# Two of the four weight-block sums of each seven-product slot made by adding loads instead of VectorE

## What is computed

```
for l in range(2):
    x = x + rms_norm(concat(conv, retention, moba, pool) @ w_out[l], attn_post_g[l])
    h = rms_norm(x, ffn_pre_g[l])
    f = silu(h @ w_gate[l]) * (h @ w_up[l])          # 1024 -> 2816, twice
    x = x + rms_norm(f @ w_down[l], ffn_post_g[l])
```

## Time and profile before

| | us |
|---|---|
| median of 3 runs | 1066.26 |
| profiled execution, its own time | 1066.48 |
| its span | 1064.7 |
| PE busy | 1044.1 (98%) |
| DVE busy | 797.5 (75%) |
| ACT busy | 498.3 (47%) |
| POOL busy | 5.2 (0%) |
| DMA queue of SP, share of 16 engines | 31.6% |

### The profile page before, as it was taken

The page is one execution under the profiler, slowest core; times in us unless marked ns, Lnnn a source line. Parts: engine busy times, 40 slices in busy tenths (PEclk is TensorE's granted clock), DMA queues, the critical chain, the costliest instruction groups (busy, mean ns, idle before and its releaser), DMA issues.

```text
span 1064.7 us, 19739 instructions
## 1 busy us (share of the span) xinstructions
PE 1044.1 (98%) x7894; PEld 776.4 (73%) x7894; DVE 797.5 (75%) x1605; ACT 498.3 (47%) x928; POOL 5.2 (0%) x18
## 2 busy tenths in 40 slices
PE   8999999999999999999999999999999999999997
PEld 5988895587888887444488888747878888864443
DVE  6999988989899987222679888898889999761014
ACT  5545454645555666122244463465555555651000
POOL 1000000000000000000000000000000000000000
PEclk9999999999999999999999999999999999999999
DMA  9612311222333546332032140223133333560001
GB/s 338 194 64 81 118 64 57 82 79 81 118 120 120 159 121 220 135 119 79 1 107 93 41 145 15 80 80 119 41 100 113 109 136 119 165 214 18 1 20 60
DMA packets 58187, 109.84 MB, mean 103 GB/s; under 512 B 7024, under 2 KB 7280, under 8 KB 57968
## 3 DMA queue, kind: packets, MB, share of 16 engines
q1 hardware_dynamic: 58096, 108.58, 31.6%
HBM read 106.46 MB, written 2.10 MB: 102 GB/s over the span
## 4 chain that ended last, share of the span: by engine, by line
PE 88%; DVE 7%; ACT 3%; issue 1%; DMA 1%; SPq 0%; ACTq 0%; DVEq 0%
PE ps L565 52%; PE ps L672 28%; PE ps L569 3%; DVE ring L1391 2%; PE ps L831 1%; ACT ring L901 1%; PE ps L815 1%; DVE E L1505 1%; DVE hT L1513 1%; PE ps L750 1%; DMA xs<-x_dram 1%; DVE ps L1470 0%; PE ps L735 0%; ACT gbc L901 0%; PE ps L792 0%
## 5 line engine op out<-in xcount | busy, mean ns | idle before, releaser
L565 PE MATMUL ps<-ring,U 128*128 128x512 f16 x1440 | 313.4, 379 | 0.0
L1391 DVE SCALAR_TENSOR_TENSOR ring<-raw,ring 128x512 f16<-128x512 f32 (+1 forms) x300 | 210.2, 744 | 89.9 <-ACT ring L901 89.9
L565 PEld LDWEIGHTS ps<-ring,U 128*128 128x128 f16 x1440 | 140.8, 98 | 166.7 <-issue 0.3
L901 ACT ACTIVATE ring<-raw 128x512 f16<-128x512 f32 (+1 forms) x300 | 181.0, 670 | 83.6 <-PE ps L565 77.1
L565 PE MATMUL ps<-hT,ring 128*128 128x256 f16 (+1 forms) x1632 | 195.3, 279 | 0.3 <-DVE hT L1513 0.3
L565 PEld LDWEIGHTS ps<-hT,ring 128*128 128x128 f16 x1632 | 159.3, 98 | 29.4 <-DVE hT L1513 0.6
L672 PE MATMUL ps<-E,ring 128*128 128x256 f16 x1224 | 145.7, 273 | 3.8 <-ACT ps L901 3.8
L672 PE MATMUL ps<-hT,ring 128*128 128x256 f16 x1224 | 145.4, 273 | 0.0
L565 PE MATMUL ps<-ring,hT 128*128 128x256 f16 x1152 | 134.8, 275 | 0.7 <-DVE hT L1513 0.7
L672 PEld LDWEIGHTS ps<-E,ring 128*128 128x128 f16 x1224 | 117.8, 98 | 20.6 <-ACT ps L901 5.4
L672 PEld LDWEIGHTS ps<-hT,ring 128*128 128x128 f16 x1224 | 119.8, 98 | 13.8
(11 more groups left out here) (134 smaller groups left out, 857.7 us busy)
## 6 DMA issues: line engine op xcount, KB each, us to landing
raw<-weights_dram SPq DMA_DIRECT2D x368, 256.0 KB, 2.9
gbc<-gains_dram SPq DMA_DIRECT2D x8, 512.0 KB, 6.4
xs<-x_dram SPq DMA_DIRECT2D x4, 512.0 KB, 6.5
U<-weights_dram SPq DMA_DIRECT2D x8, 256.0 KB, 7.4
out_dram<-xs SPq DMA_DIRECT2D x8, 256.0 KB, 2.0
cst<-consts_dram SPq DMA_DIRECT2D x1, 1296.0 KB, 12.0
bd<-pool_w_dram SPq DMA_DIRECT2D x8, 16.0 KB, 10.0
par<-params_dram SPq DMA_DIRECT2D x1, 76.0 KB, 6.3
```

The costliest lines, as they stand in the source:

```text
L565: ins = mm(dst, st, mv_, start=first and i == 0, stop=last and i == 2, **kw)
L901: return A(dst, src, ACT.Copy, scale=scale)
L1391: V.scalar_tensor_tensor(out=at[1], in0=src, scalar=W_SCALE, in1=at[0], op0=ALU.mult, op1=ALU.subtract).then_inc(lo_split, 1)
```

## The change

In each fast slot, X1 and X2 are no longer made by DVE. X1: after part B has landed in its place in `raw`, GpSimd issues a load of part A from DRAM onto the same place with an add (`accum_op`). X2: SP loads part B a second time, into one of four new places at the end of `raw`; when it has landed, GpSimd issues a load of part C onto it with an add. X3 and X4 stay on DVE, each 512 columns, and use the two other new places; `xsum` is gone. X3 now stands after lo0 (ahead of lo1), and X4 after lo1 (ahead of lo2). ACT's hi2 waits for both adding loads, and hi3 for X4. Since B's place now holds X1 until lo2, `FREES` says that it is free after lo2; the places of C and D stay as they were, free after lo1, but SP comes to them after B. The buffer `sink`, to which ScalarE writes squares that nobody reads, moves into a buffer that is idle then, and the scratch for GpSimd's DMA descriptors grows from 256 to 1024.

```diff
-FREES = ((0, 1, 2, 3), (0, 0, 1, 1))
+FREES = ((0, 1, 2, 3), (0, 2, 1, 1))
...
-        raw = sb("raw", [P, NRAW, RAW])
+        raw = sb("raw", [P, NRAW + 4, RAW])
...
+        def x12_home(n):
+            a = (PARTS * n - EARLY) % NRAW // PARTS
+            return PARTS * a + 1, NRAW + a
...
                 sp.dma_start(dst, weights[n, :, :]).then_inc(landed, 16)
+                if n % PARTS == 1 and fast(n // PARTS):
+                    i = FAST_NO[n // PARTS]
+                    if i >= 2:
+                        sp.wait_ge(lo_split, PARTS * FAST_SLOTS[i - 2] + 3)
+                    sp.dma_start(raw[:, x12_home(n // PARTS)[1], :], weights[n, :, :]).then_inc(x2_in[i % 2], 16)
...
+            for i, n in enumerate(FAST_SLOTS):
+                x1, x2 = x12_home(n)
+                _, landed, value = raw_home(PARTS * n + 1)
+                pool.wait_ge(landed, value)
+                nc.gpsimd.dma_start(raw[:, x1, :], weights[PARTS * n, :, :],
+                                    accum_op=ALU.add).then_inc(x1_sum[i % 2], 16)
+                pool.wait_ge(x2_in[i % 2], 16 * (i // 2 + 1))
+                nc.gpsimd.dma_start(raw[:, x2, :], weights[PARTS * n + 2, :, :],
+                                    accum_op=ALU.add).then_inc(x2_sum[i % 2], 16)
...
-                    act.wait_ge(x_sum, 3 * FAST_NO[n] + (1 if part == 2 else 3))
+                    if part == 2:
+                        for sums in (x1_sum, x2_sum):
+                            act.wait_ge(sums[FAST_NO[n] % 2], 16 * (FAST_NO[n] // 2 + 1))
+                    else:
+                        act.wait_ge(x_sum, 2 * FAST_NO[n] + 2)
...
             def weight_sums(n, step):
...
                 if step == 0:
-                    V.tensor_tensor(xsum[:, 0:2, :], raw[:, r:r + 2, :], raw[:, r + 1:r + 3, :],
+                    if i:
+                        dve.wait_ge(lo_split, PARTS * FAST_SLOTS[i - 1] + 4)
+                    dve.wait_ge(x1_sum[i % 2], 16 * (i // 2 + 1))
+                    V.tensor_tensor(raw[:, NRAW + 2, :], raw[:, r + 1, :], raw[:, r + 2, :], ALU.add).then_inc(x_sum, 1)
+                else:
+                    dve.wait_ge(x_sum, 2 * i + 1)
+                    V.tensor_tensor(raw[:, NRAW + 3, :], raw[:, NRAW + 2, :], raw[:, r + 3, :],
                                     ALU.add).then_inc(x_sum, 1)
-                elif step == 1:
-                    V.tensor_tensor(xsum[:, 2, :], xsum[:, 0, :], raw[:, r + 2, :], ALU.add).then_inc(x_sum, 1)
-                else:
-                    V.tensor_tensor(xsum[:, 3, :], xsum[:, 2, :], raw[:, r + 3, :], ALU.add).then_inc(x_sum, 1)
...
-                if fast(slot) and part == 0:
+                if fast(slot) and part == 1:
                     weight_sums(slot, 0)
+                if fast(slot) and part == 2:
                     weight_sums(slot, 1)
-                if fast(slot) and part == 1:
-                    weight_sums(slot, 2)
```

More of the change, by code:

```diff
@@ L197, in trunk_program @@
         gbc = sb("gbc", [P, 2, DM])
-        sink = sb("sink", [P, DM], BF16)
         gt_w = sb("gt", [P, 2 * HALF])
@@ L201, in trunk_program @@
         zeros = gt_w[:, :].bitcast(F16)
-        raw = sb("raw", [P, NRAW, RAW])
+        raw = sb("raw", [P, NRAW + 4, RAW])
         ring = sb("ring", [P, QUADS, 2, RAW], F16)
-        xsum = sb("xsum", [P, 4, RAW])
         U = sb("U", [P, FT * S])
@@ L271, in trunk_program @@
               for w in (E[:, 0:DM], xn[0], xn[1], Z[:, 0:DM])]
+        sink = hb_w[:, CW - 1:CW - 1 + DM // 2].bitcast(BF16)
         u_w, v_w = gt_w[:, 0:HALF], gt_w[:, HALF:2 * HALF]
@@ L381, in trunk_program @@
         x_sum = sem("x_sum")
+        x2_in = [sem(f"x2_in{i}") for i in range(2)]
+        x1_sum = [sem(f"x1_sum{i}") for i in range(2)]
+        x2_sum = [sem(f"x2_sum{i}") for i in range(2)]
         p1_ps = sem("p1_ps")
@@ L472, in raw_pair, with x12_pair @@
             return raw[:, at:at + 2, :]
+        def x12_home(n):
+            a = (PARTS * n - EARLY) % NRAW // PARTS
+            return PARTS * a + 1, NRAW + a
+        def x12_pair(n):
+            x1, x2 = x12_home(n)
+            return raw[:, x1:x2 + 1:x2 - x1, :]
         def raw_freed(n):
@@ L1166, in split_hi_chunk @@
                 else:
-                    act.wait_ge(x_sum, 3 * FAST_NO[n] + (1 if part == 2 else 3))
-                    copy(quads2(n, Q_X1 if part == 2 else Q_X3, 0), xsum[:, 2 * part - 4:2 * part - 2, :],
-                         W_SCALE).then_inc(hi_split, 1)
+                    if part == 2:
[3 more added lines that the diff above has]
+                        act.wait_ge(x_sum, 2 * FAST_NO[n] + 2)
+                    copy(quads2(n, Q_X1 if part == 2 else Q_X3, 0),
+                         x12_pair(n) if part == 2 else raw[:, NRAW + 2:NRAW + 4, :], W_SCALE).then_inc(hi_split, 1)
             def split_hi(*slots):
@@ L1351, in weight_sums @@
             def weight_sums(n, step):
-                base, i = PARTS * n, 3 * FAST_NO[n]
+                base, i = PARTS * n, FAST_NO[n]
                 r = (base - EARLY) % NRAW
-                if i and step < 2:
-                    dve.wait_ge(lo_split, PARTS * FAST_SLOTS[i // 3 - 1] + 3 + step)
+                _, landed, value = raw_home(base + 2 + step)
+                dve.wait_ge(landed, value)
                 if step == 0:
-                    for part in range(3):
-                        _, landed, value = raw_home(base + part)
-                        dve.wait_ge(landed, value)
-                    V.tensor_tensor(xsum[:, 0:2, :], raw[:, r:r + 2, :], raw[:, r + 1:r + 3, :],
-                                    ALU.add).then_inc(x_sum, 1)
-                elif step == 1:
-                    dve.wait_ge(x_sum, i + 1)
-                    V.tensor_tensor(xsum[:, 2, :], xsum[:, 0, :], raw[:, r + 2, :], ALU.add).then_inc(x_sum, 1)
-                else:
-                    _, landed, value = raw_home(base + 3)
-                    dve.wait_ge(landed, value)
-                    dve.wait_ge(x_sum, i + 2)
-                    V.tensor_tensor(xsum[:, 3, :], xsum[:, 2, :], raw[:, r + 3, :], ALU.add).then_inc(x_sum, 1)
+                    if i:
[5 more added lines that the diff above has]
+                    V.tensor_tensor(raw[:, NRAW + 3, :], raw[:, NRAW + 2, :], raw[:, r + 3, :],
+                                    ALU.add).then_inc(x_sum, 1)
             def split_lo_part(slot, part):
@@ L1388, in split_lo_part @@
                 else:
-                    src = xsum[:, 2 * part - 4:2 * part - 2, :]
+                    src = x12_pair(slot) if part == 2 else raw[:, NRAW + 2:NRAW + 4, :]
                     at = [quads2(slot, Q_X1 if part == 2 else Q_X3, p) for p in range(2)]
@@ L2042 @@
               "pool_w": np.ascontiguousarray(pool_w), "consts": constants()}
-    nc = bacc.Bacc("TRN2", target_bir_lowering=False, num_devices=1, dynamic_dma_scratch_size=256)
+    nc = bacc.Bacc("TRN2", target_bir_lowering=False, num_devices=1, dynamic_dma_scratch_size=1024)
     aps = [nc.dram_tensor(f"{n}_dram", a.shape, mybir.dt.from_np(a.dtype), kind="ExternalInput").ap()
```

## The result

| | before | after |
|---|---|---|
| median, us | 1066.45 (14 runs, 1066.06 to 1067.21) | 1068.20 (14 runs, 1066.31 to 1069.88) |
| ratio of the two | | 1.0017, 95% interval 1.0009 to 1.0025 |
| profiled execution, us | 1066.48 | 1068.87 |
| its span, us | 1064.7 | 1067.1 |

The time lies in the predicted range and inside the 0.2% that had been named as no change. It is 1.5 us over the forecast of 1066.7, and the runs spread three times as wide as before.

A forecast was written before the change was run, and what follows sets the result against it. PE, busy 98% of the span, was taken as the bound, so DVE's relief counts only where PE idles. +1.96 - 1.2 - 0.33 = +0.4 us gave a median of 1066.7 us, range 1064.6 to 1072.

The forecast's parts named there:

- Ordinary windows and the adding loads at 0: In ordinary 9.17 us windows, DVE's saved time gains nothing, X4's move costs nothing, and the adding loads stay hidden: 0.
- The two-slot window at +1.96: In the one window with two new slots, X4 delays hi3 and `p1_copy`; PE's wait grows from 1.70 to 3.7 us.
- The tops at -1.2 and -0.33: At the feed-forward part's top, PE's waits behind DVE shrink by 1.2 us in layer 2, 0.33 us in layer 1.
- so PE goes on 1.96 us later: Last step for the two-slot window: `p1_copy` starts at 909.15 instead of 907.19, delaying PE by 1.96 us.
- The late sums: Rival, chance 0.15: hi2 waits for X2 and PE behind it, over 28 windows; 1097 or 1195 us.
- The stall does not grow: Rival, chance 0.08: hi3's wait in the two-slot window costs nothing, the two gains stand alone; 1064.7 us.
- The small loss in ordinary windows: Rival, chance 0.07: slowed X4 or late hi2 costs 0.2 us in some 28 windows, +5.6; 1072 us.

The follow-up runs named there:

- e3: The changed kernel without GpSimd's adding loads, X1 and X2 left as copies of part B: 1068.88 us, ratio 1.0025.
- e4: The changed kernel with the adding load of X1 made twice, the second after the first has landed: 1128.77 and 1138.94 us, ratio 1.0634.
- e1: The changed kernel with X3 and X4 both made ahead of lo0, adding loads kept: 1064.75 us, ratio 0.9986.
- e2: The kernel before, without adding loads, with X4 moved from ahead of lo1 to ahead of lo2: 1069.61 us, ratio 1.0037.
- e8: The changed kernel itself run again, for a second profile: 1067.84 us, ratio 1.0016.
- e5: The changed kernel with X3, X4 ahead of lo0 and, in windows with two new slots, ACT's `p1_copy` after two hi chunks, not four: 1060.81 us, ratio 0.9949.
- e7: The changed kernel with X4 right behind X3, both ahead of lo1 and behind lo0: 1066.51 us, ratio 0.9998.

## Why the prediction was right, and what it left out

**Ordinary windows and the adding loads at 0: right.** Windows stay at 9.17 us. X2 was forecast about 5 us early. In the trace of after, B's load is issued at 343.50, the adding loads at 346.80 and 347.53, they land in 6.1 us, so near 353.6, and hi2 starts at 357.24: 3.6 us early. e3 shows that they cost nothing, e4 that the room is less than one more such load.

**The two-slot window at +1.96: right for the wait, +1.91 in the profile.** e1 and e2 show the cause from both sides: with the loads and X4 early it is absent, without the loads and with X4 late it is present.

**The tops at -1.2 and -0.33: right,** -1.24 and -0.33 in the profile.

**What was left out** is the step "so PE goes on 1.96 us later". A wait of PE was priced at its own length only. After this wait TensorE ran its next two or three products in part at the lower clock: 1.67 us in the first profile, 2.77 in e8. That one missing term is as large as the mis-forecast (1.5 us in the median), and four times the forecast's own sum of +0.4. That the time still lay in the range owes something to its width: from 1064.6 to 1072 us it had room for a term of this size. The fall probably makes most of the wider spread as well: e5, which has no wait for ACT, spreads by 0.7 us. This is argued and not shown run by run; two runs of e2 with the same mean clock of 0.997 lie 1.7 us apart. The Trainium skill (TensorE: Matmul & The Clock Gate, "Part 1: The HAM clock gate (the "warmup" mystery)") says that an idle TensorE goes to 1.2 GHz and that activity releases it again; the granted clock of 0.86 and 0.79 behind the wait agrees, and the rule would have put the missing term on the right side of the sum. The prediction says nothing of the clock. Behind the 1.70 us of the two-slot window it stayed at 1.00 before, but the same trace has the fall at the start, at 0.83 in the row above: a look at the granted clock there would have shown that a wait can cost more than its length.

**Rivals.** The late sums did not come here, though the cover was thinner than the forecast (3.6 us and not 5); e4 shows the mechanism, and that its price left out the clock. "The stall does not grow" was forecast at 1064.7 us; e1, which makes it so by moving X4, came to 1064.75. The small loss in ordinary windows did not occur.

**Open.** What decides whether the clock falls in an execution after one and the same wait. Some tenths also come from the start, where the transposes of the second norm begin between 11.43 (e7) and 12.59 us (after); between before and after it is the landing of an input that moved, by 0.55 us. No run isolates that.

## What to carry over

When an instruction is taken off a busy engine, write down the new place of those that stay: VectorE became 38 us less busy here, which was worth 1.5 us, while one sum moved behind two other instructions cost 1.9 us and more. An engine that is 98% busy gains from other engines' relief only at its own few waits, so list these first, and look for what stands ahead of the released instruction there; putting the matmul's copy ahead of two splits won twice what the whole change could. Price a wait of TensorE above its length where the traces show the granted clock falling behind such waits: here behind 2.07 us in one profile of two, and behind 3.35 to 3.61 us in four of five.

## Hardware behaviour not expected

- TensorE's clock after a wait of 2.07 us: 12 matmuls of 256 columns in 1.48 us in one execution, in 1.87 and then 2.77 us in another of the same kernel. Behind the 1.70 us of the two-slot window neither of the two profiles (before, e1) shows a fall; at the start of the program it fell after waits of 1.29 and 0.69 us (e7).
- In e4, where PE waits for ACT 23 times, the granted clock's mean over 300 to 400 us was 0.93, and PE's busy time grew by 23.5 us for the same matmuls, half as much as its waits for ACT (48.0 us).
- An adding load of 256 KB takes 6.1 us to land, a plain one beside it 3.5 us (2.9 before), and 2.1 times the DMA engines' time per byte.
